# Up projection of a float32 trunk kernel: both parts of hT in one 512-column matmul, the gated product and the rest of gT on VectorE

## The chip, the cores and the metric

The kernel runs on one core of one Trainium2 chip. The metric is device time in microseconds (us). Before the change it is 1369.4 us, the median of three runs (1368.85 to 1369.75).

## The reference

Four residual layers run over 256 tokens of width 1024, all in float32. Each has an attention mixer (three kinds), a gated MLP with a causal depthwise convolution of width 3, and a gate with a per-layer embedding. The change touches the MLP:

```python
D_FF, CONV_WIDTH = 2816, 3
def conv_ffn(h, w_up, conv_w, conv_b, w_down):
    u = h @ w_up                                   # (256, 1024) @ (1024, 5632)
    u = lax.conv_general_dilated(                  # causal, depthwise, width 3
        u, conv_w[:, None, :], window_strides=(1,), padding=[(CONV_WIDTH - 1, 0)],
        dimension_numbers=('NWC', 'WIO', 'NWC'), feature_group_count=2 * D_FF) + conv_b
    gate, up = u[..., :D_FF], u[..., D_FF:]
    return (jax.nn.silu(gate) * up) @ w_down

# in the layer loop
x = x + conv_ffn(rms_norm(x, ffn_norm[i]), w_up[i], conv_w[i], conv_b[i], w_down[i])
```

## The kernel before, in words

Every float32 operand of a matmul is split into two parts, a rounded one (`_hi`, type fp32r) and the rest (`_lo`, the value minus the rounded one). A product is three matmuls into the same PSUM bank: hi by hi, hi by lo and lo by hi.

All weights stand in one list of "units" of 128 x 2048 elements, read in the order of use. SyncE loads them in halves of 128 x 1024 into the ring `w_raw` (4 halves). ScalarE makes `w_hi` of a half (L441, `split_hi`), VectorE makes `w_lo` (L744, `split_lo`), each into a ring of 4 units. While TensorE uses unit u, these two split unit u+4. `lo_ready` tells TensorE that a unit is there and SyncE that a raw half is free. `unit_used` counts the units that TensorE has finished.

The up projection of a layer is 22 up units (`up_unit` on each engine). A unit makes 128 gate columns and 128 up columns of u, transposed, for all 256 tokens: TensorE goes over 2 sides (gate, up) and 8 chunks of the width, with three matmuls of 256 columns for each (L1296 to L1298), 48 in all, the gate's into the first half of one PSUM bank and the up's into the second half. Four banks are used in turn (`up_bank`), so unit u only waits for the convolution of unit u-4 (`conv_done`).

Behind TensorE a unit goes through these steps:

- ScalarE: the last tap with the bias, from PSUM, into `gate_c` (L713) and `up_c` (L715); then the two halves of the split of unit u+4; the silu on `gate_c` (L719); the rounding to `gT_hi` (L721).
- VectorE: the two other taps of the gate and of the up side, from PSUM (L1108, 4 instructions); then two halves of the split of unit u+4.
- GpSimd: the product of `gate_c` and `up_c` (L1282), then the rest, product minus `gT_hi`, to `gT_lo` (L1284).

Each engine works its instructions off in the order of the program. The order around the change is written out by hand; `over_units` turns it into a loop of four units a turn, with the last two units of a layer behind the loop, and with `peel` the first four units are written out ahead of it as well. Inside such a loop counts and addresses come from registers. After the up units the down projection takes 11 units, again with 512-column matmuls (L1320, L1335), on VectorE and ScalarE only splits stand beside it.

Of the kernel before, what the change touches and what calls it, by code (L numbers as in the profile page):

```python
# [17 lines left out]
F32 = mybir.dt.float32  # L18
# [144 lines left out]
def trunk(nc, weights, x_in, p_in, gains, smalls, gainT_in, bf_in, conv, wf_in, rel_in, ident_in, consts_in, out):  # L163
    with ExitStack() as ctx:
# [9 lines left out]
        hT_hi = sb("hT_hi", [P, KC, SEQ], F32R)  # L174
        hT_lo = sb("hT_lo", [P, KC, SEQ], F32R)
# [66 lines left out]
        bank = [ctx.enter_context(nc.psum_tensor(f"bank{i}", [P, 512], F32)) for i in range(8)]  # L242
# [31 lines left out]
        def up_bank(L, slot):  # L274
            return aux[(slot - FIRST_UP[L]) % RING]
# [72 lines left out]
        gainT_ready = sem("gainT_ready")  # L348
        conv_first = sem("conv_first")
# [81 lines left out]
        def _(act):  # L431
# [20 lines left out]

            def split_looped(u, slot, half, k):
                split_hi(u + RING, slot, lambda q: (half(q)[0], half(q)[1] + 2 * RING // RAW))
# [68 lines left out]
            for L in range(DEPTH):  # L523
# [182 lines left out]

                def up_unit(u, slot, half, k):
                    b = slot % 2
                    act.wait_ge(unit_used, u + 1)
                    c = conv_sb[:, L, k, :]  # L710
                    if not isinstance(k, int) or FC * L + k >= 2:
                        act.wait_ge(gT_ready, k + (FC * L - 1))
                    nc.scalar.activation(gate_c[:, b, :], up_bank(L, slot)[:, 0:SEQ], ACT.Identity,  # L713
                                         bias=c[:, 3:4], scale=c[:, 2:3]).then_inc(conv_first, 1)
                    nc.scalar.activation(up_c[:, b, :], up_bank(L, slot)[:, SEQ:2 * SEQ], ACT.Identity,  # L715
                                         bias=c[:, 7:8], scale=c[:, 6:7]).then_inc(conv_first, 1)
                    split_looped(u, slot, half, k)
                    act.wait_ge(conv_done, k + (FC * L + 1))
                    nc.scalar.activation(gate_c[:, b, :], gate_c[:, b, :], ACT.Silu).then_inc(silu_done, 1)  # L719
                    act.wait_ge(prod_done, k + (FC * L + 1))  # L720
                    nc.scalar.activation(gT_hi[:, k, :], gate_c[:, b, :], ACT.Copy).then_inc(gT_hi_ready, 1)  # L721

                act.preload_act_table(ACT.Silu)
                over_units(act, FIRST_UP[L], FC, up_unit, peel=L == 0)
# [11 lines left out]
        def _(dve):  # L736
# [19 lines left out]
            def split_looped(u, slot, half, k):  # L756
                split_lo(u + RING, slot, half)
# [83 lines left out]
            for L in range(DEPTH):  # L841
# [254 lines left out]

                def up_unit(u, slot, half, k):
                    b = slot % 2
                    c = conv_sb[:, L, k, :]

                    dve.wait_ge(conv_first, k * 2 + (2 * FC * L + 2))
                    for tap in (1, 0):
                        lag = 2 - tap
                        for side, buf in ((0, gate_c), (1, up_c)):
                            if tap == 0:

                                dve.wait_ge(conv_tap, k * 2 + (2 * FC * L + side + 1))
                            ins = nc.vector.scalar_tensor_tensor(  # L1108
                                buf[:, b, lag:SEQ], up_bank(L, slot)[:, side * SEQ:side * SEQ + SEQ - lag],
                                c[:, 4 * side + tap:4 * side + tap + 1], buf[:, b, lag:SEQ], ALU.mult, ALU.add)  # L1110
                            if tap == 1:
                                ins.then_inc(conv_tap, 1)
                    ins.then_inc(conv_done, 1)
                    split_looped(u, slot, half, k)

                over_units(dve, FIRST_UP[L], FC, up_unit)
# [10 lines left out]
        def _(pool):  # L1127
# [41 lines left out]
            for L in range(DEPTH):  # L1169
# [108 lines left out]

                def up_unit(u, slot, half, k):
                    b = slot % 2  # L1280
                    pool.wait_ge(silu_done, k + (FC * L + 1))
                    nc.gpsimd.tensor_tensor(gate_c[:, b, :], gate_c[:, b, :], up_c[:, b, :], ALU.mult).then_inc(prod_done, 1)  # L1282
                    pool.wait_ge(gT_hi_ready, k + (FC * L + 1))
                    nc.gpsimd.tensor_tensor(gT_lo[:, k, :], gate_c[:, b, :], gT_hi[:, k, :].bitcast(F32), ALU.subtract).then_inc(gT_ready, 1)  # L1284

                over_units(pool, FIRST_UP[L], FC, up_unit)
# [6 lines left out]
        def _(pe):  # L1293
# [60 lines left out]
            for L in range(DEPTH):  # L1354
# [326 lines left out]
```

## Time and profile before

| what | us |
|---|---|
| median of 3 runs | 1369.4 |
| the profiled execution | 1371.7 |
| its span, first to last instruction | 1369.9 |
| TensorE matmul busy, whole span | 1317.6 (96%) |
| VectorE busy | 971.1 (71%) |
| ScalarE busy | 828.6 (60%) |
| GpSimd busy | 417.6 (30%) |
| up projection of the first layer, 149.6 to 276.5 | 126.9 |

The busy time of an engine is what its instructions took, without waits. The granted TensorE clock is a share of full speed. Matmuls overlap each other in the trace (one of 256 columns is shown as 0.28 us long, and the next starts 0.12 us after it), so the pace of TensorE is read from the starts, not from the durations. On VectorE and ScalarE the start of an instruction can lie up to 0.1 us before the shown end of the one ahead of it, too.

### The profile page before, as it was taken

To read this page: it belongs to the slowest core of one execution; us is meant where nothing else is said; L and a number is where in the kernel's file an instruction comes from. 1 tells how busy PE (TensorE), PEld (TensorE's weight loads), DVE (VectorE), ACT (ScalarE), POOL (GpSimd) and SP (SyncE) were. 2 spreads that over 40 slices of the span, in tenths; PEclk is the share of its full clock that TensorE was granted. 3 is DMA by queue.
4 is the path that set the end of the run, shared out by engine and by line. 5 is a ranking of instruction groups with operands and counts; after the bars stand their busy time and mean duration, and the time that the engine had idled before them with its cause. 6 is when DMAs were issued, how large, how long until landed. Compare 5 with 4: busy or idle time off the path is not lost.

```text
span 1369.9 us, 24686 instructions
## 1 busy us (share of the span) xinstructions
PE 1317.6 (96%) x8340; PEld 1174.1 (86%) x8340; DVE 971.1 (71%) x1531; ACT 828.6 (60%) x1469; POOL 417.6 (30%) x523
## 2 busy tenths in 40 slices
PE   5999999999999999999996799999999999999998
PEld 4878999988788899998875689998887788999887
DVE  4677877755777777774588687776476787777635
ACT  4676666644568666663465666665365786666533
POOL 3541233310265123330037313332014520333200
PEclk9999999999999999999998899999999999999999
DMA  8533655555664456656543155556556335555651
GB/s 289 165 129 102 206 184 182 181 194 177 198 226 136 151 177 184 184 184 201 174 156 108 47 170 184 184 184 194 175 177 200 123 110 184 182 181 179 195 184 62
DMA packets 64311, 232.89 MB, mean 170 GB/s; under 512 B 7312, under 2 KB 7440, under 8 KB 64240
## 3 DMA queue, kind: packets, MB, share of 16 engines
q1 hardware_dynamic: 61344, 221.87, 50.1%
q0 software_dynamic: 2896, 10.08, 2.6%
q8 instruction: 44, 0.72, 0.2%
q14 instruction: 27, 0.22, 0.1%
HBM read 230.87 MB, written 1.05 MB: 169 GB/s over the span
## 4 chain that ended last, share of the span: by engine, by line
PE 80%; DVE 9%; ACT 4%; POOL 3%; issue 2%; DMA 2%; SPq 0%; POOLq 0%; DVEq 0%; ACTq 0%
PE bank L1320 23%; PE bank L1296 17%; PE bank L1297 16%; PE bank L1298 16%; DVE w_lo L744 4%; PE bank L1335 3%; DMA w_raw<-weights 2%; PE bank L1465 2%; PE bank L1488 1%; DVE tok L787 1%; ACT w_hi L441 1%; ACT tok L464 1%; ACT hT_hi L472 1%; PE bank L1385 1%; POOL hrstd L1141 1%
## 5 line engine op out<-in xcount | busy, mean ns | idle before, releaser
L744 DVE TENSOR_TENSOR w_lo<-w_raw,w_hi 128x1024 fp32r<-128x1024 f32 x418 | 556.3, 1367 | 124.3 <-ACT w_hi L441 123.3
L441 ACT ACTIVATE w_hi<-w_raw 128x1024 fp32r<-128x1024 f32 x418 | 422.2, 1056 | 150.4 <-PE bank L1320 117.4
L1296 PE MATMUL bank<-hT_hi,w_hi 128*128 128x256 f32 x1408 | 398.7, 283 | 2.1 <-DVE hT_lo L795 2.1
L1298 PE MATMUL bank<-hT_hi,w_lo 128*128 128x256 f32 x1408 | 398.4, 283 | 0.0
L1297 PE MATMUL bank<-hT_lo,w_hi 128*128 128x256 f32 x1408 | 398.4, 283 | 0.0
L1296 PEld LDWEIGHTS bank<-hT_hi,w_hi 128*128 128x128 f32 x1408 | 270.3, 192 | 3.7 <-issue 3.7
L1298 PEld LDWEIGHTS bank<-hT_hi,w_lo 128*128 128x128 f32 x1408 | 270.3, 192 | 0.0
L1297 PEld LDWEIGHTS bank<-hT_lo,w_hi 128*128 128x128 f32 x1408 | 270.3, 192 | 0.0
L1282 POOL TENSOR_TENSOR gate_c<-gate_c,up_c 128x256 f32<-128x256 f32 x88 | 105.1, 1194 | 288.6 <-ACT gate_c L719 288.6
L1108 DVE SCALAR_TENSOR_TENSOR gate_c<-bank,conv_sb,gate_c 128x255 f32<-128x255 f32 (+1 forms) x176 | 84.1, 478 | 116.6 <-ACT up_c L715 116.6
L1296 PE MATMUL bank<-w_hi,hT_hi 128*128 128x512 f32 (+1 forms) x336 | 135.2, 402 | 7.9 <-DVE w_lo L744 4.2
L1297 PE MATMUL bank<-w_lo,hT_hi 128*128 128x512 f32 (+1 forms) x336 | 130.8, 389 | 0.0
L1298 PE MATMUL bank<-w_hi,hT_lo 128*128 128x512 f32 (+1 forms) x336 | 130.6, 389 | 0.0
L1146 POOL TENSOR_TENSOR ssq<-ssq 128x1 f32<-128x1 f32 x24 | 7.5, 315 | 378.5 <-ACT tok L464 378.5
L721 ACT ACTIVATE gT_hi<-gate_c 128x256 f32 (+1 forms) x88 | 36.8, 419 | 122.2 <-POOL gate_c L1282 122.2
L1284 POOL TENSOR_TENSOR gT_lo<-gate_c,gT_hi 128x256 f32 (+1 forms) x88 | 84.4, 959 | 63.5 <-ACT gT_hi L721 63.5
L1320 PE MATMUL bank<-w_hi,gT_hi 128*128 128x512 f32 x320 | 98.6, 389 | 0.0
L1320 PE MATMUL bank<-w_lo,gT_hi 128*128 128x512 f32 x320 | 98.6, 389 | 0.0
L1320 PE MATMUL bank<-w_hi,gT_lo 128*128 128x512 f32 x320 | 98.5, 389 | 0.0
L713 ACT ACTIVATE gate_c<-bank,conv_sb 128x256 f32<-128x256 f32 x88 | 49.7, 565 | 67.1 <-PE bank L1298 67.1
L1296 PEld LDWEIGHTS bank<-w_hi,hT_hi 128*128 128x128 f32 x336 | 63.9, 190 | 24.7 <-DVE w_lo L744 5.9
L1108 DVE SCALAR_TENSOR_TENSOR up_c<-bank,conv_sb,up_c 128x255 f32<-128x255 f32 (+1 forms) x176 | 83.3, 474 | 0.1
(159 smaller groups left out, 2096.8 us busy)
## 6 DMA issues: line engine op xcount, KB each, us to landing
w_raw<-weights SPq DMA_DIRECT2D x418, 512.0 KB, 4.1
gain<-gains POOLq DMA_DIRECT2D x11, 512.0 KB, 4.9
rel<-rel_in POOLq DMA_DIRECT2D x8, 256.0 KB, 3.6
x<-x_in SPq DMA_DIRECT2D x2, 512.0 KB, 6.3
p_raw<-p_in POOLq DMA_DIRECT2D x4, 256.0 KB, 5.2
out<-x SPq DMA_DIRECT2D x4, 256.0 KB, 2.6
gain<-gains SPq DMA_DIRECT2D x1, 512.0 KB, 6.8
consts<-consts_in POOLq DMA_DIRECT2D x1, 392.0 KB, 3.6
```

The lines of the kernel that those rows point to most:

```text
L441: nc.scalar.activation(w_hi[:, slot, q * HALF:(q + 1) * HALF], w_raw[:, raw, :], ACT.Copy).then_inc(hi_ready, 1)
L713: nc.scalar.activation(gate_c[:, b, :], up_bank(L, slot)[:, 0:SEQ], ACT.Identity, bias=c[:, 3:4], scale=c[:, 2:3]).then_inc(conv_first, 1)
L721: nc.scalar.activation(gT_hi[:, k, :], gate_c[:, b, :], ACT.Copy).then_inc(gT_hi_ready, 1)
L744: nc.vector.tensor_tensor(w_lo[:, slot, cols], w_raw[:, half(q)[0], :], w_hi[:, slot, cols].bitcast(F32), ALU.subtract).then_inc(lo_ready, 1)
L1108: ins = nc.vector.scalar_tensor_tensor(buf[:, b, lag:SEQ], up_bank(L, slot)[:, side * SEQ:side * SEQ + SEQ - lag], c[:, 4 * side + tap:4 * ...
L1282: nc.gpsimd.tensor_tensor(gate_c[:, b, :], gate_c[:, b, :], up_c[:, b, :], ALU.mult).then_inc(prod_done, 1)
L1284: nc.gpsimd.tensor_tensor(gT_lo[:, k, :], gate_c[:, b, :], gT_hi[:, k, :].bitcast(F32), ALU.subtract).then_inc(gT_ready, 1)
L1296: nc.tensor.matmul(out_ap, l_hi, r_hi, start=start, stop=False, skip_group_check=True)
L1297: nc.tensor.matmul(out_ap, l_hi, r_lo, start=False, stop=False, skip_group_check=True)
L1298: return nc.tensor.matmul(out_ap, l_lo, r_hi, start=False, stop=stop, skip_group_check=True)
L1320: last = nc.tensor.matmul(banks[2 * t + b][:, :], l[:, c, ts], w[:, slot, col:col + 512], start=(c == 0 and l is left_hi and w is w_hi), s ...
L1335: last = nc.tensor.matmul(banks[2 * t + b][:, :], l[:, c, ts], w[:, slot, col:col + 512], start=False, stop=(j == 1 and l is left_lo), ski ...
```

## The change

The two parts of hT become one tile `hT` of [128, 8, 2, 256]. For each side and chunk one matmul of 512 columns multiplies `w_hi` with both parts at once: the first 256 columns of the bank get hi by hi, the last 256 hi by lo. A second matmul of 256 columns adds `w_lo` by `hT_hi` to the first 256. A unit is then 32 matmuls and fills two banks, so that two units instead of four fit into the four banks. ScalarE copies the last 256 columns of both banks to `cross_c`, VectorE adds the first 256 of both (`both_c`), and the taps read `both_c` in SBUF. TensorE waits for the sum of unit u-2 (`up_sum`). The product and the rest of gT go from GpSimd to VectorE, and with the rounding on ScalarE they stand in the turn of the next unit.

```diff
+        hT = sb("hT", [P, KC, 2, SEQ], F32R)
+        hT_hi, hT_lo = hT[:, :, 0, :], hT[:, :, 1, :]
+            cross_c = sb("cross_c", [P, 2, SEQ], F32, ffn)
+            both_c = sb("both_c", [P, 2, SEQ], F32, ffn)
...
-        def up_bank(L, slot):
-            return aux[(slot - FIRST_UP[L]) % RING]
+        def up_banks(L, slot):
+            b = 4 + 2 * ((slot - FIRST_UP[L]) % 2)
+            return psum[:, b:b + 2, :]
... ScalarE
+                def round_g(b, count, k):
+                    act.wait_ge(prod_done, count)
+                    nc.scalar.activation(gT_hi[:, k, :], gate_c[:, b, :], ACT.Copy).then_inc(gT_hi_ready, 1)
                 def up_unit(u, slot, half, k):
                     b = slot % 2
                     act.wait_ge(unit_used, u + 1)
+                    if not isinstance(k, int) or FC * L + k >= 1:
+                        act.wait_ge(up_sum, k + FC * L)
+                    nc.scalar.activation(cross_c[:], up_banks(L, slot)[:, :, SEQ:2 * SEQ], ACT.Copy).then_inc(cross_out, 1)
+                    if not isinstance(k, int) or k:
+                        round_g(1 - b, k + FC * L, k + -1)
+                    split_hi(u + RING, slot, later(half), halves=(0,))
+                    act.wait_ge(up_sum, k + (FC * L + 1))
...
-                    nc.scalar.activation(gate_c[:, b, :], up_bank(L, slot)[:, 0:SEQ], ACT.Identity,
+                    nc.scalar.activation(gate_c[:, b, :], both_c[:, 0, :], ACT.Identity,
...
-                    nc.scalar.activation(up_c[:, b, :], up_bank(L, slot)[:, SEQ:2 * SEQ], ACT.Identity,
+                    nc.scalar.activation(up_c[:, b, :], both_c[:, 1, :], ACT.Identity,
...
-                    split_looped(u, slot, half, k)
+                    split_hi(u + RING, slot, later(half), halves=(1,))
                     act.wait_ge(conv_done, k + (FC * L + 1))
                     nc.scalar.activation(gate_c[:, b, :], gate_c[:, b, :], ACT.Silu).then_inc(silu_done, 1)
-                    act.wait_ge(prod_done, k + (FC * L + 1))
-                    nc.scalar.activation(gT_hi[:, k, :], gate_c[:, b, :], ACT.Copy).then_inc(gT_hi_ready, 1)
... VectorE
+                def product(b, count):
+                    dve.wait_ge(silu_done, count)
+                    nc.vector.tensor_tensor(gate_c[:, b, :], gate_c[:, b, :], up_c[:, b, :], ALU.mult).then_inc(prod_done, 1)
+                def rest_g(b, count, k):
+                    dve.wait_ge(gT_hi_ready, count)
+                    nc.vector.tensor_tensor(gT_lo[:, k, :], gate_c[:, b, :], gT_hi[:, k, :].bitcast(F32),
+                                            ALU.subtract).then_inc(gT_ready, 1)
                 def up_unit(u, slot, half, k):
...
+                    dve.wait_ge(cross_out, k + (FC * L + 1))
+                    nc.vector.tensor_tensor(both_c[:], up_banks(L, slot)[:, :, 0:SEQ], cross_c[:], ALU.add).then_inc(up_sum, 1)
+                    if not isinstance(k, int) or k:
+                        product(1 - b, k + FC * L)
+                    split_lo(u + RING, slot, half, halves=(0,))
+                    if not isinstance(k, int) or k:
+                        rest_g(1 - b, k + FC * L, k + -1)
                     dve.wait_ge(conv_first, k * 2 + (2 * FC * L + 2))
... the four taps, now from both_c
-                    split_looped(u, slot, half, k)
-                over_units(dve, FIRST_UP[L], FC, up_unit)
+                    split_lo(u + RING, slot, half, halves=(1,))
+                over_units(dve, FIRST_UP[L], FC, up_unit, peel=True)
+                last = (FIRST_UP[L] + FC - 1) % RING % 2
+                product(last, FC * (L + 1))
+                rest_g(last, FC * (L + 1), FC - 1)
... GpSimd: up_unit goes
... TensorE
-                    if not isinstance(k, int) or FC * L + k >= RING:
-                        pe.wait_ge(conv_done, k + (FC * L + 1 - RING))
+                    if not isinstance(k, int) or FC * L + k >= 2:
+                        pe.wait_ge(up_sum, k + (FC * L - 1))
...
-                            last = three(up_bank(L, slot)[:, side * SEQ:(side + 1) * SEQ], w_hi[:, slot, col], w_lo[:, slot, col],
-                                         hT_hi[:, c, :], hT_lo[:, c, :], c == 0, c == KC - 1)
+                            into = up_banks(L, slot)[:, side, :]
+                            nc.tensor.matmul(into, w_hi[:, slot, col], hT[:, c, :, :], start=c == 0, stop=c == KC - 1,
+                                             skip_group_check=True)
+                            last = nc.tensor.matmul(into[:, 0:SEQ], w_lo[:, slot, col], hT_hi[:, c, :], start=False,
+                                                    stop=c == KC - 1, skip_group_check=True)
```

On ScalarE, in the first layer, the second up unit before is this (names are output<-input, and what the instruction waits for):

```order
L713 ACTIVATE gate_c<-bank,conv_sb 128x256 [waits unit_used]
L715 ACTIVATE up_c<-bank,conv_sb 128x256
L441 ACTIVATE w_hi<-w_raw 128x1024 [waits unit_used,raw_landed0]
L441 ACTIVATE w_hi<-w_raw 128x1024 [waits raw_landed1]
L719 ACTIVATE gate_c<-gate_c 128x256 [waits conv_done]
L721 ACTIVATE gT_hi<-gate_c 128x256 [waits prod_done]
```

In the changed kernel the same unit on ScalarE is:

```order
L727 ACTIVATE cross_c<-bank 128x512 [waits up_sum,unit_used]
L720 ACTIVATE gT_hi<-gate_c 128x256 [waits prod_done]
L448 ACTIVATE w_hi<-w_raw 128x1024 [waits unit_used,raw_landed0]
L735 ACTIVATE gate_c<-both_c,conv_sb 128x256 [waits up_sum]
L737 ACTIVATE up_c<-both_c,conv_sb 128x256
L448 ACTIVATE w_hi<-w_raw 128x1024 [waits unit_used,raw_landed1]
L741 ACTIVATE gate_c<-gate_c 128x256 [waits conv_done]
```

A copy out of PSUM comes first, the rounding (of the unit before) stands ahead of the first half of the split, and the second half stands behind the taps of ScalarE.

On VectorE the body of the loop over the up units before is this, for one unit (ISA and REGISTER_ALU rows are register steps of the loop):

```order
L1108 ISA [waits conv_first]
L1108 SCALAR_TENSOR_TENSOR gate_c<-bank,conv_sb,gate_c 128x255
L1108 ISA
L1108 SCALAR_TENSOR_TENSOR up_c<-bank,conv_sb,up_c 128x255
L1107 REGISTER_ALU
L1108 ISA [waits conv_tap]
L1108 SCALAR_TENSOR_TENSOR gate_c<-bank,conv_sb,gate_c 128x254
L1108 ISA [waits conv_tap]
L1108 SCALAR_TENSOR_TENSOR up_c<-bank,conv_sb,up_c 128x254
L742 ISA
L744 TENSOR_TENSOR w_lo<-w_raw,w_hi 128x1024 [waits hi_ready]
```

In the changed kernel VectorE's second up unit, written out ahead of the loop, is:

```order
L1133 TENSOR_TENSOR both_c<-bank,cross_c 128x512 [waits cross_out]
L1121 TENSOR_TENSOR gate_c<-gate_c,up_c 128x256 [waits silu_done]
L765 TENSOR_TENSOR w_lo<-w_raw,w_hi 128x1024 [waits hi_ready]
L1126 TENSOR_TENSOR gT_lo<-gate_c,gT_hi 128x256 [waits gT_hi_ready]
L1146 SCALAR_TENSOR_TENSOR gate_c<-both_c,conv_sb,gate_c 128x255 [waits conv_first]
L1146 SCALAR_TENSOR_TENSOR up_c<-both_c,conv_sb,up_c 128x255
L1146 SCALAR_TENSOR_TENSOR gate_c<-both_c,conv_sb,gate_c 128x254 [waits conv_tap]
L1146 SCALAR_TENSOR_TENSOR up_c<-both_c,conv_sb,up_c 128x254 [waits conv_tap]
L765 TENSOR_TENSOR w_lo<-w_raw,w_hi 128x1024 [waits hi_ready]
```

The sum and the product now stand ahead of the first half of the split, and the rest of gT ahead of the taps; before, both halves of the split followed the taps.

## Rows read from the trace of the kernel before

**Rows 1.** The page: busy time by engine, and granted clock in 40 slices.

```profile
PE 1317.6 (96%) x8340; PEld 1174.1 (86%) x8340; DVE 971.1 (71%) x1531; ACT 828.6 (60%) x1469; POOL 417.6 (30%) x523
PEclk9999999999999999999998899999999999999999
```

**Rows 2.** Windows (PE, PEld, DVE, ACT, POOL busy, clock, DMA), up projection, first layer.

```profile
149.60:276.50 126.90, 126.83 (x1057) 126.86 (x1058) 98.89 (x132) 80.86 (x129) 45.03 (x42) 1.00 0.59 184
```

**Rows 3.** Timeline of PE (start, duration): first, middle and last of these up units.

```profile
149.67 0.36 PE L1296 MATMUL bank<-hT_hi,w_hi 128*128 128x256 f32 x1 [0.53 <-DVE hT_lo L795]
...
200.13 0.28 PE L1296 MATMUL bank<-hT_hi,w_hi 128*128 128x256 f32 x1
200.25 0.28 PE L1297 MATMUL bank<-hT_lo,w_hi 128*128 128x256 f32 x1
...
276.45 0.63 PE L1320 MATMUL bank<-w_hi,gT_hi 128*128 128x512 f32 x2
```

**Rows 4.** Timeline of ACT, one up unit inside the loop and the next one's start.

```profile
230.78 0.57 ACT L713 ACTIVATE gate_c<-bank,conv_sb 128x256 f32<-128x256 f32 x1 [0.58 <-PE bank L1298]
231.25 0.56 ACT L715 ACTIVATE up_c<-bank,conv_sb 128x256 f32<-128x256 f32 x1
231.70 2.00 ACT L441 ACTIVATE w_hi<-w_raw 128x1024 fp32r<-128x1024 f32 x2
233.65 0.42 ACT L719 ACTIVATE gate_c<-gate_c 128x256 f32<-128x256 f32 x1
235.48 0.42 ACT L721 ACTIVATE gT_hi<-gate_c 128x256 f32 x1 [1.41 <-POOL gate_c L1282]
236.54 0.56 ACT L713 ACTIVATE gate_c<-bank,conv_sb 128x256 f32<-128x256 f32 x1 [0.64 <-PE bank L1298]
```

**Rows 5.** Timeline of DVE, the same unit.

```profile
231.96 0.48 DVE L1108 SCALAR_TENSOR_TENSOR gate_c<-bank,conv_sb,gate_c 128x255 f32<-128x255 f32 x1 [1.23 <-ACT up_c L715]
232.36 0.47 DVE L1108 SCALAR_TENSOR_TENSOR up_c<-bank,conv_sb,up_c 128x255 f32<-128x255 f32 x1
...
233.54 2.89 DVE L744 TENSOR_TENSOR w_lo<-w_raw,w_hi 128x1024 fp32r<-128x1024 f32 x2
```

**Rows 6.** Timeline of PE, 512-column matmuls of the down projection.

```profile
325.44 0.39 PE L1335 MATMUL bank<-w_hi,gT_hi 128*128 128x512 f32 x1
...
325.67 0.39 PE L1335 MATMUL bank<-w_lo,gT_hi 128*128 128x512 f32 x1
```

**Rows 7.** Groups by line and shape (busy us, mean ns), whole span.

```profile
L441 ACT ACTIVATE w_hi<-w_raw 128x1024 fp32r<-128x1024 f32 x418 | 422.2, 1056 | 150.4 <-PE bank L1320 117.4 <-DMA w_raw<-weights 23.3 <-PE bank L1298 9.4
L472 ACT ACTIVATE hT_hi<-bank 128x512 fp32r<-128x512 f32 x48 | 26.3, 604 | 29.7 <-PE bank L1306 29.7
L839 DVE TENSOR_TENSOR wf_lo<-wf_raw,wf_hi 128x256 fp32r<-128x256 f32 x1 | 0.4, 418 | 0.0
```

**Rows 8.** Timeline of DVE outside the up projection, GpSimd doing nothing.

```profile
139.51 0.68 DVE L764 TENSOR_TENSOR x<-x,bank 128x512 f32<-128x512 f32 x1
140.11 1.22 DVE L744 TENSOR_TENSOR w_lo<-w_raw,w_hi 128x1024 fp32r<-128x1024 f32 x1
141.25 1.38 DVE L764 TENSOR_TENSOR x<-x,bank 128x512 f32<-128x512 f32 x2
142.54 1.41 DVE L787 SCALAR_TENSOR_TENSOR tok<-x,rstd,gain 128x512 f32<-128x512 f32 x2
...
283.21 2.36 DVE L744 TENSOR_TENSOR w_lo<-w_raw,w_hi 128x1024 fp32r<-128x1024 f32 x2 [1.04 <-ACT w_hi L441]
288.65 2.36 DVE L744 TENSOR_TENSOR w_lo<-w_raw,w_hi 128x1024 fp32r<-128x1024 f32 x2 [3.08 <-ACT w_hi L441]
```

**Rows 9.** Windows (columns as in Rows 2) of the third layer's attention.

```profile
725.00:730.00 5.00, 3.90 (x19) 2.62 (x17) 5.00 (x7) 2.49 (x3) 4.60 (x3) 1.00 0.47 143
...
735.00:740.00 5.00, 0.12 (x4) 0.00 (x0) 3.21 (x14) 3.13 (x10) 3.19 (x5) 0.81 0.24 95
740.00:745.00 5.00, 3.97 (x22) 3.35 (x22) 2.80 (x10) 3.26 (x11) 2.53 (x5) 0.50 0.00 0
```

More of the change, by code:

```diff
@@ L173, in trunk @@
         tok = sb("tok", [P, TT, D])
-        hT_hi = sb("hT_hi", [P, KC, SEQ], F32R)
-        hT_lo = sb("hT_lo", [P, KC, SEQ], F32R)
+        hT = sb("hT", [P, KC, 2, SEQ], F32R)
+        hT_hi, hT_lo = hT[:, :, 0, :], hT[:, :, 1, :]
         gain = sb("gain", [P, D])
@@ L239, in sc @@
             return sc_tok[:, slot, :] if slot < 4 else sc_gain[:, slot - 4, :]
-        bank = [ctx.enter_context(nc.psum_tensor(f"bank{i}", [P, 512], F32)) for i in range(8)]
+        psum = ctx.enter_context(nc.psum_tensor("bank", [P, 8, 512], F32))
+        bank = [psum[:, i, :] for i in range(8)]
         acc, aux = bank[:4], bank[4:]
@@ L348, in trunk @@
         gainT_ready = sem("gainT_ready")
+        cross_out = sem("cross_out")
+        up_sum = sem("up_sum")
         conv_first = sem("conv_first")
@@ L451, in split_half, with later @@
                 split_hi(u, u % RING, half_of(u), halves=(j % 2,))
+            def later(half):
+                return lambda q: (half(q)[0], half(q)[1] + 2 * RING // RAW)
             def split_looped(u, slot, half, k):
-                split_hi(u + RING, slot, lambda q: (half(q)[0], half(q)[1] + 2 * RING // RAW))
+                split_hi(u + RING, slot, later(half))
             def square(n, t):
@@ L712, in up_unit @@
                         act.wait_ge(gT_ready, k + (FC * L - 1))
-                    nc.scalar.activation(gate_c[:, b, :], up_bank(L, slot)[:, 0:SEQ], ACT.Identity,
+                    nc.scalar.activation(gate_c[:, b, :], both_c[:, 0, :], ACT.Identity,
                                          bias=c[:, 3:4], scale=c[:, 2:3]).then_inc(conv_first, 1)
-                    nc.scalar.activation(up_c[:, b, :], up_bank(L, slot)[:, SEQ:2 * SEQ], ACT.Identity,
+                    nc.scalar.activation(up_c[:, b, :], both_c[:, 1, :], ACT.Identity,
                                          bias=c[:, 7:8], scale=c[:, 6:7]).then_inc(conv_first, 1)
-                    split_looped(u, slot, half, k)
+                    split_hi(u + RING, slot, later(half), halves=(1,))
                     act.wait_ge(conv_done, k + (FC * L + 1))
                     nc.scalar.activation(gate_c[:, b, :], gate_c[:, b, :], ACT.Silu).then_inc(silu_done, 1)
-                    act.wait_ge(prod_done, k + (FC * L + 1))
-                    nc.scalar.activation(gT_hi[:, k, :], gate_c[:, b, :], ACT.Copy).then_inc(gT_hi_ready, 1)
                 act.preload_act_table(ACT.Silu)
-                over_units(act, FIRST_UP[L], FC, up_unit, peel=L == 0)
+                over_units(act, FIRST_UP[L], FC, up_unit, peel=True)
+                round_g((FIRST_UP[L] + FC - 1) % RING % 2, FC * (L + 1), FC - 1)
                 over_units(act, FIRST_DOWN[L], DOWN_UNITS - DOWN_TAIL, split_looped)
@@ L1108, in up_unit @@
                             ins = nc.vector.scalar_tensor_tensor(
-                                buf[:, b, lag:SEQ], up_bank(L, slot)[:, side * SEQ:side * SEQ + SEQ - lag],
+                                buf[:, b, lag:SEQ], both_c[:, side, 0:SEQ - lag],
                                 c[:, 4 * side + tap:4 * side + tap + 1], buf[:, b, lag:SEQ], ALU.mult, ALU.add)
@@ L1276, in _ @@
                 load_gain(3 * L + 2)
[L1279 to L1286, printed above, removed]
                 norm_rstd(3 * L + 2)
```

## The prediction

> **What bounds the kernel now.** I read the page first: TensorE is busy for 96% of the span at a clock that is full almost everywhere [rows 1], so nothing but TensorE's own work and its few gaps sets the time. The stage that is changed comes next, by windows: in the first layer's up projection TensorE is busy 126.83 of 126.90 us at granted clock 1.00 (2.4 GHz), VectorE 98.89, ScalarE 80.86, GpSimd 45.03 [rows 2]. Then its timeline. A 256-column matmul starts every 0.12 us; the stage runs from 149.67 to 276.45, 126.78 us for 22 units, 5.76 a unit, which is 48 x 0.12 [rows 3]. TensorE has no gap there, so the stage ends when the matmuls end. Last, what stands behind it: ScalarE and VectorE take up one unit each 5.76 us because TensorE delivers it so, ScalarE waiting 0.64 us for TensorE and 1.41 for GpSimd [rows 4], VectorE 1.23 for ScalarE [rows 5]. That slack is what the change draws on: the question is whether the new, longer chain between ScalarE and VectorE still closes within one TensorE unit.
>
> **TensorE's part.** A 512-column matmul starts 0.23 us after the one before (two rows: 325.44, 325.67 [rows 6]); against 0.12 for 256 columns the columns cost 0.11 per 256 and the instruction itself some 0.01. To a finer digit: a down unit has 24 of them and VectorE's splits, which follow it, come 5.44 us apart (283.21, 288.65 [rows 8]), so 0.227 each. That gives 16 x 0.227 + 16 x 0.12 = 5.55 us for a unit in place of 5.76: 0.21 us less, and 18.5 us less over 88 units, if TensorE is never kept waiting.
>
> A rule speaks against even that. By the Trainium skill, page "TensorE: Matmul & The Clock Gate", section "Wait — 56ns, not 53.3ns?", a warm matmul costs its columns at 2.4 GHz and about 2.5 ns more; 16 matmuls saved would then be 0.04 us a unit and 3.5 us in all (an estimate from that page). The trace disagrees: 0.12 us for 256 columns is 13 ns above their 107 ns.
>
> **ScalarE and VectorE: the cycle.** With the new order each unit u passes back and forth between the two in one line, because each engine's queue is strict. I start it where VectorE starts the sum of unit u, and give each step the time until the next can start:
>
> - the sum, 512 columns, one source in PSUM: as `x<-x,bank`, whose follower starts 0.60 later [rows 8]: 0.60
> - the product of unit u-1, 256 columns out of SBUF. The nearest row is a 256-column subtraction of 0.418 us [rows 7]; ScalarE waits for its end: 0.42
> - handing over to ScalarE. Inside the loop a register step stands between wait and operation. `up_c` ends at 231.81 and VectorE's tap starts at 231.96 [rows 4, 5]: 0.15
> - the rounding of unit u-1, 0.42 long, its follower able to start some 0.10 earlier (gate_c is 0.57 long, up_c starts after 0.47 [rows 4]): 0.32
> - the first half's `w_hi`, 1.056 [rows 7], whose end VectorE awaits, and 0.04 for the hand-over: 1.10
> - the first half's `w_lo`, start to next start 1.14 (140.11 to 141.25, GpSimd idle [rows 8]): 1.14
> - the rest of gT of unit u-1: 0.42 less the 0.08 by which a follower starts early (0.68 against 0.60 [rows 8]): 0.34
> - four taps, 231.96 to 233.54 [rows 5]: 1.58. ScalarE's two taps are long done by then: they start when `w_hi` ends and need 1.0 of the 1.48 us
> - the second half's `w_lo`: 1.14. Then the sum of unit u+1 can start.
>
> The sum is 0.60 + 0.42 + 0.15 + 0.32 + 1.10 + 1.14 + 0.34 + 1.58 + 1.14 = 6.79 us. The way over ScalarE is as long: from the end of the last tap 0.04, silu 0.33, the copy to cross_c 0.60 (as `hT_hi<-bank`, 0.604 [rows 7]) and 0.04 put the next sum at 6.74. Where units are written out ahead of the loop, the register step falls away and the cycle is 6.67.
>
> VectorE's own work in it, start to start, is 5.14 us (0.60 + 0.34 + 1.14 + 0.34 + 1.58 + 1.14) and would fit under 5.55. What does not fit is the other 1.65 us (6.79 - 5.14), in which VectorE stands between the product and `w_lo` while ScalarE rounds and makes `w_hi` of half 0; nothing else in VectorE's queue can go ahead. Before, the splits of both engines came after the taps and overlapped. GpSimd, whose 45 us per stage [rows 2] are freed, was never the bound; its going gives VectorE's pair of `w_lo` 2.36 us where it took 2.89 [rows 8, 5], and that is counted above.
>
> So from the second unit on TensorE waits for `up_sum` of unit u-2, and that comes every 6.79 us, not every 5.55. Two banks a unit leave room for two units only.
>
> **The stage.** Unit 1 leaves TensorE at 11.10. Its results reach ScalarE about 0.3 later (unit 0 before: 149.67 + 5.76 = 155.43, and in the loop ScalarE's start lies some 0.3 to 0.5 behind a unit's end), the copy takes 0.60, so sum 1 starts at 12.0. Sum 19 starts 18 cycles later, 3 of 6.67 and 15 of 6.79: 133.9. It takes 0.68, TensorE takes it up 0.15 later and needs 5.55 for unit 21: 140.3 us. Before it was 126.78: 13.5 us more in each of four layers, 54 us.
>
> **What hides the rest.** The two last units' silu, product and rest trail TensorE by up to two cycles, but the down projection's first unit needs only the first two units of gT, and its weights come from splits made in up units 18 to 21. Down unit 2 needs the second half of unit 20, ready about 147; TensorE reaches it at 140.3 + 10.9 = 151.2. Down unit 3 needs unit 21's, about 154 against 156.6. The lag is made good there, where each engine has 3 us spare a unit (VectorE takes 2.36 of 5.44 [rows 8]). Loads ask for less per us than before, so they cost nothing. Copies, norms and attention are unchanged.
>
> The profiled execution has a span of 1369.9 us and was 1371.7 itself, against a median of 1369.4. Its span would be 1424. From the median: 1369.4 + 54 = 1423 us.
>
> **Bounds of the unknown terms.** The trace of before has no tap that reads SBUF. From PSUM a tap's follower starts after 0.40 for 255 columns [rows 5]; the scalar_tensor_tensor out of SBUF has 1.41 - 0.74 = 0.67 for 512 [rows 8]. At 1.05 us per 1000 columns (1.14 for 1024 against 0.60 for 512 [rows 8]) both leave 0.13: no gain. I take 0.39 to 0.40, with 0.45 as the upper end (a whole tap without overlap is 0.47).
>
> The Trainium skill, page "VectorE: DVE Perf Modes", section "The TRN2 errata", has 58 cycles beside the columns out of SBUF and 120 out of PSUM. By it four taps would be 0.26 us shorter, the cycle 6.53 and the time 1404 (an estimate from that page); the rows say otherwise for this form.
>
> Hand-overs run from 0.04 to 0.15, five in the cycle or on its equal branch. Low end: all short and the 256-column operations 0.05 shorter each: cycle 6.5. High end: all long, taps 0.45: 7.15. 72 cycles in all make that -21 and +26 us: 1402 to 1449.
>
> **Rivals.**
>
> *TensorE keeps the bound.* If the cycle closed within 5.55 us, the matmuls' saving would show: 1369.4 - 18.5 = 1351. For it speaks that VectorE's work alone is 5.14. Against it, 1.65 us of waiting that the order forces. Chance 0.04.
>
> *TensorE waits, but the cheaper matmuls pay for it.* The stage is 12.0 + 18 cycles + 0.68 + 0.15 + 5.55, which equals the old 126.78 at a cycle of 6.02. If two of the hand-overs and the start of `w_hi` overlapped so far that 0.77 us fell out of the one wait ahead of `w_lo`, the time would be that of before, 1369. Chance 0.02.
>
> *TensorE's clock falls too.* TensorE would stand still 1.2 us in every 6.8. The trace has a stretch of 3.90 busy in 5 us at clock 1.00, and 0.50 (1.2 GHz) only behind a stretch with 0.12 us of work in five [rows 9]. At 1.2 GHz a unit would take about 11 us, more than the cycle; if a tenth of the stage ran so, 9 units would cost 4.3 more each, 39 us: 1462. Chance 0.05.
>
> *The cycle is longer than I sum.* Loop branches each fourth unit, or a half of a load late now that the halves are asked for apart: 7.3 us gives 1423 + 72 x 0.5 = 1459. Chance 0.06.
>
> **How the numbers follow.** The forecast has 0.83, and its own range is that of the bounds. The low end stands at 1402; the high one I leave at 1449, which leaves the two slow rivals and the two fast ones, 0.17, outside. A difference of 0.2%, 2.7 us, can be told from none. Faster 0.04, same 0.02, slower 0.94.
>
> **What would show it.** In the changed profile the up stage of layer one should be about 140 us, with TensorE busy near 83% in it, waiting once a unit, 1.2 us, for VectorE's `both_c`. VectorE's longest wait should stand before the first `w_lo` of a unit, about 1.6 us, on ScalarE's `w_hi`; the pair's halves should be 1.2 us each; successive `both_c` 6.7 to 6.8 us apart; 512-column matmuls 0.227 apart where they don't wait. The down stage should be as long as before. The forecast is wrong if `both_c` comes each 5.6 us, if TensorE's clock is below 1 in the stage, or if matmuls of a unit take other than 5.55 us.

## The result, and the profile after

The changed kernel takes 1425.6 us, the median of 4 runs (1423.2 to 1429.7), against 1369.6 before: a ratio of 1.040, 95% interval 1.037 to 1.044. It is slower by 56 us; 54 were forecast. The profiled execution was the slowest of the four, 1429.7, with a span (first to last instruction) of 1427.9.

The page of the changed kernel, busy time by engine and granted clock in 40 slices, as in [rows 1]:

```profile
PE 1323.1 (93%) x6932; PEld 1099.8 (77%) x6932; DVE 1035.2 (72%) x1795; ACT 876.8 (61%) x1557; POOL 230.1 (16%) x347
PEclk9999999999999999999998899999999999999999
```

TensorE has 1408 fewer matmuls and a smaller share of busy time; the clock is as before. VectorE's share has hardly risen, 71 to 72%: a reader who looks only at shares finds no engine that could be the new bound. The view of waits (who waited for whom: us in total, times, longest) finds it:

```profile
DVE w_lo L765 <- ACT w_hi L448: 216.3, 160, 3.8
ACT gate_c L741 <- DVE up_c L1146: 110.7, 88, 1.5
ACT gT_hi L720 <- DVE gate_c L1121: 107.6, 88, 1.5
...
PEld bank L1599 <- DVE both_c L1133: 57.4, 49, 1.4
...
PE bank L1599 <- DVE both_c L1133: 41.8, 49, 1.1
```

ScalarE waits for VectorE twice in each of the 88 units, VectorE for ScalarE once in nearly each (the 160 of the first line hold other stages too; 20 lie in the first up stage of 22 units), and TensorE waits for VectorE's sum `both_c`. Each stop of TensorE stands in this view twice, at the weight load and at the matmul behind it: the 49 and 49 are 49 stops. Eleven more are booked on a `w_lo`, but they too end just behind a sum (one at 235.19 behind 235.08) and are waits for it. That makes 60 stops, 15 a layer.

VectorE's timeline, one unit in the loop and the two next sums (start, duration, idle before):

```profile
227.66 0.68 DVE L1133 TENSOR_TENSOR both_c<-bank,cross_c 128x512 f32<-128x512 f32 x1
228.26 0.42 DVE L1121 TENSOR_TENSOR gate_c<-gate_c,up_c 128x256 f32<-128x256 f32 x1
230.21 1.23 DVE L765 TENSOR_TENSOR w_lo<-w_raw,w_hi 128x1024 fp32r<-128x1024 f32 x1 [1.53 <-ACT w_hi L448]
231.35 0.42 DVE L1126 TENSOR_TENSOR gT_lo<-gate_c,gT_hi 128x256 f32 x1
231.69 0.48 DVE L1146 SCALAR_TENSOR_TENSOR gate_c<-both_c,conv_sb,gate_c 128x255 f32<-128x255 f32 x1
232.08 0.48 DVE L1146 SCALAR_TENSOR_TENSOR up_c<-both_c,conv_sb,up_c 128x255 f32<-128x255 f32 x1
...
233.27 1.22 DVE L765 TENSOR_TENSOR w_lo<-w_raw,w_hi 128x1024 fp32r<-128x1024 f32 x1
234.40 0.68 DVE L1133 TENSOR_TENSOR both_c<-bank,cross_c 128x512 f32<-128x512 f32 x1
...
241.23 0.69 DVE L1133 TENSOR_TENSOR both_c<-bank,cross_c 128x512 f32<-128x512 f32 x1
```

ScalarE beside it:

```profile
228.81 0.42 ACT L720 ACTIVATE gT_hi<-gate_c 128x256 f32 x1 [1.26 <-DVE gate_c L1121]
229.13 1.04 ACT L448 ACTIVATE w_hi<-w_raw 128x1024 fp32r<-128x1024 f32 x1
230.08 0.59 ACT L735 ACTIVATE gate_c<-both_c,conv_sb 128x256 f32<-128x256 f32 x1
...
233.38 0.42 ACT L741 ACTIVATE gate_c<-gate_c 128x256 f32<-128x256 f32 x1 [1.27 <-DVE up_c L1146]
233.71 0.58 ACT L727 ACTIVATE cross_c<-bank 128x512 f32<-128x512 f32 x1
```

Read the two as one line: VectorE's product ends at 228.68, ScalarE rounds at 228.81 and makes `w_hi` from 229.13 to 230.17, VectorE makes `w_lo` at 230.21. In those 1.53 us VectorE does nothing. The way once around, from one sum to the next, is what is called the cycle here. In the loop it is by turns about 6.75 and 6.82 us, 6.65 where the units are written out, and 6.77 on average from the second sum of the layer to the twentieth; before, a unit took 5.76 [rows 3 to 5].

TensorE's timeline: the starts of two units and of the first that stops, then the end of a later unit and the start and end of the next:

```profile
182.60 0.39 PE L1599 MATMUL bank<-hT,w_hi 128*128 128x512 f32 x1
...
188.15 0.39 PE L1599 MATMUL bank<-hT,w_hi 128*128 128x512 f32 x1
...
194.22 0.50 PE L1599 MATMUL bank<-hT,w_hi 128*128 128x512 f32 x1 [0.36 <-DVE both_c L1133]
...
227.22 0.28 PE L1601 MATMUL bank<-hT,w_lo 128*128 128x256 f32 x1
228.40 0.50 PE L1599 MATMUL bank<-hT,w_hi 128*128 128x512 f32 x1 [0.90 <-DVE both_c L1133]
...
228.85 0.40 PE L1599 MATMUL bank<-hT,w_hi 128*128 128x512 f32 x1
...
233.80 0.40 PE L1599 MATMUL bank<-hT,w_hi 128*128 128x512 f32 x1
```

For seven units TensorE does not stop: it starts at 154.79, and a unit takes 5.55 us (182.60 to 188.15), as forecast. The first stop is ahead of the eighth unit, at 194.22, and from there on every unit waits for a sum. The first matmul of such a unit starts 0.06 us after the end of the sum (228.34). From 228.85 to 233.80 are 14 pairs of a 512- and a 256-column matmul, 0.354 each; 16 of them would be 5.66 us. So TensorE has two paces here, 0.347 a pair before the first stop and mostly 0.354 behind it, both at granted clock 1.00.

### The profile page after: what moved, and what is told of

The parts are those of the page before. It is cut to its first block, busy times and chain, and to the rows that moved or that the text cites. A ratio compares the mean times of both kernels' runs of the same rounds, so it can differ in the third digit from the quotient of the medians.

```text
span 1427.9 us, 21936 instructions
## 1 busy us (share of the span) xinstructions
PE 1323.1 (93%) x6932; PEld 1099.8 (77%) x6932; DVE 1035.2 (72%) x1795; ACT 876.8 (61%) x1557; POOL 230.1 (16%) x347
## 4 chain that ended last, share of the span: by engine, by line
PE 46%; DVE 26%; issue 10%; ACT 10%; POOL 3%; DMA 2%; ACTq 1%; DVEq 1%; SPq 0%; POOLq 0%
PE bank L1352 22%; DVE w_lo L765 11%; PE bank L1599 4%; PE bank L1328 4%; PE bank L1329 3%; PE bank L1330 3%; DVE gate_c L1146 3%; PE bank L1367 3%; DVE both_c L1133 3%; ACT gate_c L735 2%; DVE up_c L1146 2%; ACT up_c L737 2%; PE bank L1601 2%; ACT w_hi L448 2%; DMA w_raw<-weights 2%
## 5 line engine op out<-in xcount | busy, mean ns | idle before, releaser
L1599 PE MATMUL bank<-hT,w_hi 128*128 128x512 f32 x1408 | 501.6, 400 | 53.6 <-DVE both_c L1133 41.8
L1601 PE MATMUL bank<-hT,w_lo 128*128 128x256 f32 x1408 | 393.4, 279 | 0.0
L1599 PEld LDWEIGHTS bank<-hT,w_hi 128*128 128x128 f32 x1408 | 264.0, 188 | 133.8 <-DVE both_c L1133 57.4
L1601 PEld LDWEIGHTS bank<-hT,w_lo 128*128 128x128 f32 x1408 | 265.5, 189 | 0.0
L1328 PE MATMUL bank<-w_hi,hT 128*128 128x512 f32 (+1 forms) x336 | 136.9, 408 | 9.1 <-DVE w_lo L765 5.3
L1329 PE MATMUL bank<-w_lo,hT 128*128 128x512 f32 (+1 forms) x336 | 132.1, 393 | 0.0
L1330 PE MATMUL bank<-w_hi,hT 128*128 128x512 f32 (+1 forms) x336 | 132.1, 393 | 0.0
L1352 PE MATMUL bank<-w_hi,hT 128*128 128x512 f32 x384 | 107.6, 392 | 0.0
L1328 PEld LDWEIGHTS bank<-w_hi,hT 128*128 128x128 f32 x336 | 64.9, 193 | 26.1 <-DVE w_lo L765 7.0
L1146 DVE SCALAR_TENSOR_TENSOR up_c<-both_c,conv_sb,up_c 128x255 f32<-128x255 f32 (+1 forms) x176 | 84.1, 478 | 0.1
L1146 DVE SCALAR_TENSOR_TENSOR gate_c<-both_c,conv_sb,gate_c 128x255 f32<-128x255 f32 (+1 forms) x176 | 84.1, 478 | 0.0
L1352 PEld LDWEIGHTS bank<-w_hi,hT 128*128 128x128 f32 x384 | 70.9, 188 | 14.8
L1330 PEld LDWEIGHTS bank<-w_hi,hT 128*128 128x128 f32 x336 | 64.8, 193 | 13.7
```

Source lines behind the costliest of these rows:

```text
L1146: ins = nc.vector.scalar_tensor_tensor(buf[:, b, lag:SEQ], both_c[:, side, 0:SEQ - lag], c[:, 4 * side + tap:4 * side + tap + 1], buf[:, b ...
L1328: nc.tensor.matmul(out_ap, l_hi, r_hi, start=start, stop=False, skip_group_check=True)
L1329: nc.tensor.matmul(out_ap, l_hi, r_lo, start=False, stop=False, skip_group_check=True)
L1330: return nc.tensor.matmul(out_ap, l_lo, r_hi, start=False, stop=stop, skip_group_check=True)
L1352: last = nc.tensor.matmul(banks[2 * t + b][:, :], l[:, c, ts], w[:, slot, col:col + 512], start=(c == 0 and l is left_hi and w is w_hi), s ...
L1599: nc.tensor.matmul(into, w_hi[:, slot, col], hT[:, c, :, :], start=c == 0, stop=c == KC - 1, skip_group_check=True)
```

## The experiments

**The order, nothing else.** The changed kernel with two ScalarE steps exchanged:

```diff
+                    split_hi(u + RING, slot, later(half), halves=(0,))
                     if not isinstance(k, int) or k:
                         round_g(1 - b, k + FC * L, k + -1)
-                    split_hi(u + RING, slot, later(half), halves=(0,))
```

> The changed kernel with two ScalarE steps of an up unit exchanged: the first half's w_hi goes ahead of the rounding of the unit before. Same instructions, same banks. Theory (the one wait of VectorE between the product and w_lo makes the cycle): w_hi then runs beside VectorE's sum and product, the cycle is 0.60 + 0.34 + 1.14 + 0.34, some 0.3 of waiting for ScalarE's taps, 1.58 and 1.14, 5.4 us, less than a unit of TensorE (16 pairs at 0.354 in the changed kernel's trace, 5.66). TensorE has no gap again and the kernel is faster than the one before: 1369.5 - 4 x 22 x 0.10 = 1360 us. Rival 'VectorE and ScalarE simply have too much work': the work is the same, so 1425. Rival 'two banks a unit, two units deep': the banks are the same, so 1425.

Measured: 1357.0 us (1353.2 to 1358.2, 5 runs), 0.989 of the kernel before (0.988 to 0.991). Work, banks and instructions are those of the changed kernel, 69 us are gone, and it is 1.1% faster than the kernel before. VectorE's timeline in this kernel, and ScalarE's beside it:

```profile
225.39 0.69 DVE L1133 TENSOR_TENSOR both_c<-bank,cross_c 128x512 f32<-128x512 f32 x1
226.00 0.42 DVE L1121 TENSOR_TENSOR gate_c<-gate_c,up_c 128x256 f32<-128x256 f32 x1
226.34 1.23 DVE L765 TENSOR_TENSOR w_lo<-w_raw,w_hi 128x1024 fp32r<-128x1024 f32 x1
227.48 0.42 DVE L1126 TENSOR_TENSOR gT_lo<-gate_c,gT_hi 128x256 f32 x1
228.18 0.48 DVE L1146 SCALAR_TENSOR_TENSOR gate_c<-both_c,conv_sb,gate_c 128x255 f32<-128x255 f32 x1 [0.28 <-ACT up_c L737]
...
231.04 0.69 DVE L1133 TENSOR_TENSOR both_c<-bank,cross_c 128x512 f32<-128x512 f32 x1
```

```profile
224.76 0.60 ACT L727 ACTIVATE cross_c<-bank 128x512 f32<-128x512 f32 x1
225.25 1.05 ACT L448 ACTIVATE w_hi<-w_raw 128x1024 fp32r<-128x1024 f32 x1
226.56 0.42 ACT L720 ACTIVATE gT_hi<-gate_c 128x256 f32 x1 [0.25 <-DVE gate_c L1121]
```

ScalarE makes `w_hi` from 225.25 to 226.30, beside VectorE's sum and product. The wait ahead of `w_lo` is gone, 0.28 before the taps are left, and sums come 5.65 apart in this layer, at TensorE's pace. Windows of the up stage in this kernel, layers one and three (columns as in [rows 2]):

```profile
150.00:274.00 124.00, 123.48 (x699) 106.83 (x698) 114.94 (x193) 94.77 (x149) 0.00 (x0) 1.00 0.58 190
...
807.00:928.00 121.00, 120.72 (x697) 105.63 (x697) 113.29 (x192) 93.67 (x149) 0.00 (x0) 1.00 0.59 192
```

Neither too much work nor two units of banks costs the 56 us by itself: both are here as in the changed kernel, VectorE is busy 93% of this stage, and TensorE has no stop in it.

**One more instruction where VectorE waits, and where it doesn't.** A product of 256 columns into a spare tile, in the changed kernel. First in the gap:

```diff
+                    nc.vector.tensor_tensor(spare[:], consts[:, 0:SEQ], consts[:, 0:SEQ], ALU.mult)
                     split_lo(u + RING, slot, half, halves=(0,))
```

> The changed kernel with one more VectorE instruction a unit, a product of 256 columns into a spare tile, 0.34 us, between the product and the first half's w_lo. Theory: VectorE stands still 1.53 us there, so it costs nothing: 1425. Rival 'VectorE has too much work': 0.34 x 72 = 24 us more, 1450.

Measured: 1425.5 us (4 runs), as without it. VectorE waits 1.20 in place of 1.53. Then behind the taps:

```diff
                     ins.then_inc(conv_done, 1)
+                    nc.vector.tensor_tensor(spare[:], consts[:, 0:SEQ], consts[:, 0:SEQ], ALU.mult)
                     split_lo(u + RING, slot, half, halves=(1,))
```

> The changed kernel with the spare 256-column VectorE product a unit, but now behind the taps, ahead of the second half's w_lo, where VectorE does not wait. Theory: it lengthens the cycle by its 0.34 to 0.40 us, 18 times a layer: 1425 + 4 x 18 x 0.34 = 1450 (up to 1454). Rival 'ScalarE's branch alone makes the cycle': 1425, as with the instruction in the gap.

Measured: 1449.5 us (4 runs), 24 more. Most sums are 7.07 to 7.15 us apart in place of 6.74 to 6.83. The same instruction costs nothing in one place and its 0.34 us, 18 times in each of four layers, in the other. So the time follows the length of the cycle and not the work of VectorE.

**Product and rest alone.** The new order and VectorE's product, with 48 matmuls into four banks and the taps from PSUM as before:

```diff
-                    nc.scalar.activation(cross_c[:], up_banks(L, slot)[:, :, SEQ:2 * SEQ], ACT.Copy).then_inc(cross_out, 1)
...
-                    nc.vector.tensor_tensor(both_c[:], up_banks(L, slot)[:, :, 0:SEQ], cross_c[:], ALU.add).then_inc(up_sum, 1)
...
-                        pe.wait_ge(up_sum, k + (FC * L - 1))
+                        pe.wait_ge(conv_done, k + (FC * L + 1 - RING))
...
```

> One part of the change alone: product and rest of gT on VectorE one unit behind, in the new order; the up projection in 48 matmuls of 256 columns into four banks as before, no copy, no sum. Theory: the cycle is 0.42 + 0.15 + 0.32 + 1.10 + 1.14 + 0.34 + 1.58 + 1.14 = 6.2 us, 0.43 more than TensorE's 5.76. But a layer has only 22 units and TensorE may be four ahead: unit 21 needs the taps of unit 17, which come at about 16.4 + 16 x 6.2 = 115.4 us, before TensorE gets there at 121. So 1369.5, no change, though the cycle is too long. Rival 'a cycle longer than TensorE's unit costs its difference each time': 0.43 x 72 = 31, 1400.

Measured: 1371.1 us, 1.0006 of before (0.9995 to 1.0017). VectorE's products in its trace and the window of the first up stage:

```profile
243.43 0.42 DVE L1115 TENSOR_TENSOR gate_c<-gate_c,up_c 128x256 f32<-128x256 f32 x1
245.43 1.23 DVE L759 TENSOR_TENSOR w_lo<-w_raw,w_hi 128x1024 fp32r<-128x1024 f32 x1 [1.59 <-ACT w_hi L446]
...
249.61 0.42 DVE L1115 TENSOR_TENSOR gate_c<-gate_c,up_c 128x256 f32<-128x256 f32 x1
```

```profile
149.60:276.50 126.90, 126.37 (x1049) 125.79 (x1048) 94.59 (x161) 76.06 (x123) 0.20 (x1) 1.00 0.54 176
```

The same wait is there, 1.59 us, and the cycle is 6.18, longer than TensorE's 5.76. Yet TensorE is never stopped: four banks and the weight ring let it run ahead of a backlog of 0.42 x 20 = 8 us, and the down projection, where only splits are left, pays it back.

So the depth has its share in the 56 us, though not alone. No run gives the changed kernel room for four units. An estimate from its trace: its last up unit would then wait for its weights and not for a bank; their `w_lo` ends at 282.02 (280.80 and 1.22), and with 5.66 for the unit the stage would be 132.9 us, 6 more than before in place of 13.6.

**The matmuls alone.** 512 columns, copy and sum; product and rest on GpSimd, and the old order behind the taps:

```diff
... ScalarE
+                    split_looped(u, slot, half, k)
                     act.wait_ge(conv_done, k + (FC * L + 1))
                     nc.scalar.activation(gate_c[:, b, :], gate_c[:, b, :], ACT.Silu).then_inc(silu_done, 1)
+                    round_g(b, k + (FC * L + 1), k)
... VectorE: split_looped behind the taps; GpSimd: product and rest as before the change
```

> The other part alone: 512-column matmuls, two banks a unit, the copy to cross_c and the sum, but product and rest on GpSimd and the order behind the taps as before. Theory: ScalarE now has the cycle: copy 0.60, sum 0.72, hand-over 0.15, taps 0.95, two w_hi 1.92, silu 0.42, GpSimd's product 1.41 with its hand-overs, rounding 0.33: 6.5 us. The stage is 12.0 + 18 x 6.5 + 6.4 = 135.4, 8.6 more than before, in four layers 34: 1404 us. Rival 'moving product and rest to VectorE is what costs': 1360 to 1370.

Measured: 1503.6 us, 1.097 of before (1.096 to 1.099): 100 us above the forecast. GpSimd's and VectorE's timelines:

```profile
230.10 2.34 POOL L1312 TENSOR_TENSOR gate_c<-gate_c,up_c 128x256 f32<-128x256 f32 x1 [3.98 <-ACT gate_c L738]
```

```profile
229.49 2.35 DVE L762 TENSOR_TENSOR w_lo<-w_raw,w_hi 128x1024 fp32r<-128x1024 f32 x2
233.51 0.69 DVE L1130 TENSOR_TENSOR both_c<-bank,cross_c 128x512 f32<-128x512 f32 x1 [1.67 <-ACT cross_c L727]
...
241.29 0.69 DVE L1130 TENSOR_TENSOR both_c<-bank,cross_c 128x512 f32<-128x512 f32 x1 [1.66 <-ACT cross_c L727]
```

GpSimd's product, 1.20 us long in the kernel before (its L1282), takes 2.34 here and ends 0.60 us after VectorE's pair of `w_lo` (231.84). The cycle is 7.78 in place of 6.5. Before, the pair itself was the longer, 2.89 [rows 5]; by these lengths GpSimd then got in between its halves.

TensorE now stands still for some 2 us ahead of a unit, and its clock does not stay full. Two units in a row (columns as in [rows 2]):

```profile
218.62:226.40 7.78, 5.91 (x32) 4.89 (x32) 4.62 (x7) 4.27 (x7) 3.05 (x2) 1.00 0.37 117
226.46:234.20 7.74, 7.40 (x32) 6.12 (x32) 4.63 (x7) 4.27 (x7) 3.08 (x2) 0.78 0.43 144
```

The granted clock is 0.78 in the second, the mean of a stretch at 2.4 GHz and one at 1.2, where pairs start 0.64 us apart; before both units TensorE had stopped for about 2 us. It costs no time here: the sums stay 7.78 us apart, since the slow unit ends some 7 us before its own sum is due (233.87 against 241.29), and TensorE only waits less (0.39 us) afterwards.

For the product of GpSimd I put something small between the two `w_lo`:

```diff
                     split_lo(u + RING, slot, half, halves=(0,))
+                    nc.vector.tensor_reduce(spare[:], consts[:, 0:SEQ].rearrange("p (h d) -> p h d", d=64), AX.X, ALU.add)
                     split_lo(u + RING, slot, half, halves=(1,))
```

> The kernel with the matmuls' part alone (product on GpSimd), with a small VectorE sum over 256 columns, one SBUF source, between the two halves of w_lo; nothing else is changed. There GpSimd's product took 2.34 us in place of 1.20, until VectorE's second w_lo was over. Theory 'GpSimd is locked out of SBUF reads by VectorE's two-source instructions standing back to back': the product gets in after the first w_lo, the cycle falls by about 1.1 us, 18 x 4 x 1.1 = 79: 1425. Rival 'GpSimd is slow for another reason': 1503 or more.

Measured: 1419.2 us (4 runs). One instruction more and 84 us less:

```profile
227.86 1.20 POOL L1315 TENSOR_TENSOR gate_c<-gate_c,up_c 128x256 f32<-128x256 f32 x1 [3.79 <-ACT gate_c L739]
```

The product is back at 1.20 us, and it is VectorE's second `w_lo` that is longer now, 1.43. The Trainium skill, page "SBUF — State Buffer", section "Who interferes with whom", says that a VectorE instruction with two SBUF inputs and a GpSimd instruction that reads SBUF exclude each other for a whole instruction. The runs agree, and add that two such VectorE instructions back to back can both pass ahead of a waiting GpSimd. A VectorE instruction with two sources in the same place was not tried, so what lets GpSimd in may be the one source or just a third instruction. Why GpSimd got in between the two before, and in the first kernel of this part didn't, with the same offset of 0.61 us, is open as well.

**How much longer the cycle may be.** The kernel with `w_hi` first, and the spare product behind the taps:

> The kernel with w_hi ahead of the rounding, and the same spare product behind the taps. Its cycle was 5.65 with some 0.13 us of waiting for TensorE in it, so about 5.86 with the product. Theory: TensorE may be ahead by a start of 18.4 us against 22 units of 5.66, so cycles up to (124.5 - 18.4) / 18 = 5.89 cost nothing: 1357, no slower than without. Rival 'each 0.1 us of cycle above TensorE's unit counts in each unit': 0.2 to 0.3 x 88 = 18 to 26 us, 1375 to 1383.

Measured: 1361.3 us (1358.4 to 1362.7, 5 runs), 0.993 of before (0.992 to 0.995). VectorE's sums:

```profile
228.67 0.68 DVE L1134 TENSOR_TENSOR both_c<-bank,cross_c 128x512 f32<-128x512 f32 x1
...
234.49 0.69 DVE L1134 TENSOR_TENSOR both_c<-bank,cross_c 128x512 f32<-128x512 f32 x1
```

The cycle is 5.82, and 4 to 5 us are lost (by the ratios to the kernel before, 5), not 18 to 26. From the rounding of hT to the second down matmuls the stage is 128.65 us in the first two layers, as without the product (128.64). The third is 128.65 against 126.32, but not by the cycle: TensorE has no stop in it, its pairs start 0.353 us apart where the profile without the product has 0.347 in this layer. The start of one pair and of the sixteenth behind it, without the product and with it:

```profile
865.60 0.39 PE L1599 MATMUL bank<-hT,w_hi 128*128 128x512 f32 x1
...
871.14 0.39 PE L1599 MATMUL bank<-hT,w_hi 128*128 128x512 f32 x1
```

```profile
865.30 0.40 PE L1601 MATMUL bank<-hT,w_hi 128*128 128x512 f32 x1
...
870.95 0.40 PE L1601 MATMUL bank<-hT,w_hi 128*128 128x512 f32 x1
```

These are 16 pairs each, 5.54 and 5.65 us. Only the fourth layer, at the quicker pace, meets the limit: TensorE stops ahead of its last two units for 0.05 and 0.2 us, and the stage is 126.82 in place of 126.31. So between the two profiles 0.5 us is the cycle's and 2.3 are TensorE's pace; where the rest of the loss lies wasn't found.

**TensorE's own pace.** `w_hi` first, and a side's matmuls in two groups:

```diff
                         for c in range(KC):
                             ... the 512-column matmul
+                        for c in range(KC):
                             ... the 256-column matmul
```

> The kernel with w_hi ahead of the rounding, and TensorE's matmuls of a side in two groups: the 8 of 512 columns, then the 8 of 256, in place of pairs. In pairs a unit took 5.66 us in layers one and two and 5.54 in three and four. Theory 'going from a 256-column matmul to a 512-column one costs': 8 x 0.227 + 8 x 0.12 a side, 5.55 in all layers, 4 to 5 us less, 1352. Rival 'the pace hangs on something else of the layer': the same 1357.

Measured: 1358.1 us, 0.991 of before (0.990 to 0.993), the same as in pairs. The groups' starts in the first layer:

```profile
227.71 2.00 PE L1599 MATMUL bank<-hT,w_hi 128*128 128x512 f32 x8
229.56 1.12 PE L1603 MATMUL bank<-hT,w_lo 128*128 128x256 f32 x8
230.51 1.78 PE L1599 MATMUL bank<-hT,w_hi 128*128 128x512 f32 x7
```

8 of 512 take 1.85 us, 0.231 each, and 8 of 256 take 0.95: 5.60 a unit, and the sums come 5.59 apart in all four layers. In pairs it is 5.65 in two layers of one profile and 5.55 in the two others, so grouping lies between the two and gains nothing. The two paces of the pairs don't belong to a layer: the third is the quick one without the spare product and the slow one with it, and in the changed kernel every layer begins at 0.347 and changes where TensorE first stops. What chooses the pace wasn't found.

## Why the prediction was right, point by point

**The cycle.** Step by step, forecast and the trace after (227.66 to 234.40): sum 0.60 and 0.60; product 0.42 and 0.42; hand-over 0.15 and 0.13; rounding 0.32 and 0.32; `w_hi` with hand-over 1.10 and 1.08; `w_lo` 1.14 and 1.14; rest 0.34 and 0.34; taps 1.58 and 1.58; second `w_lo` 1.14 and 1.13. Together 6.79 and 6.74. Every price came from a row of the same shape, or a neighbour's. ScalarE's branch was nearly equal as forecast: cross_c ends at 234.29, 0.11 before the sum; at 241.20, where the loop turns over, it is the later one, and the 6.83 up to the sum at 241.23 is its.

**Taps from SBUF.** 0.39 to 0.40 from one to the next (231.69, 232.08), as from PSUM [rows 5]. The 58 against 120 cycles that the prediction cites from the Trainium skill, page "VectorE: DVE Perf Modes", section "The TRN2 errata", don't show in this form.

**The stage.** Forecast 140.3 us in the first layer; TensorE's first up matmul started at 154.79 and the first down matmul at 295.18: 140.4. The second sum started 12.0 us behind the first matmul, as forecast, and 18 cycles later came the twentieth, at 288.67. From the rounding of hT to the second down matmuls the four layers are longer by 13.6, 12.9, 13.0 and 13.2 us, together 52.8 against 54. The profiled span has another 5.1 us ahead of the first up stage: hT is rounded at 150.75 against 145.63, and in the other profiles of this study at 145.7 to 148.7, so that is a difference between executions. The medians are 56.0 us apart; the 3 us beyond the four stages have no cause shown.

**The rest hidden.** Between the stages nothing moved: from the second down matmuls to the next hT 204.5 us against 204.6, 194.5 against 194.4, 213.1 against 213.0.

**Rivals.** TensorE did not keep the bound; it did as soon as one instruction had moved. Its clock did not fall: 1.00 in the stage, with stops of about 1.1 us from the eighth unit on. The rival was not baseless, though: behind stops of 2 us, in the kernel with the matmuls alone, the granted clock fell to 0.78 in some units; there a pair at 1.2 GHz took 0.64 us, so a unit would take 10.2 and not the 11 of the prediction. The cycle was not longer than the sum.

**What was off.** Three statements of the prediction did not hold, and none of them moves the sum.

- TensorE does not wait "from the second unit on". The first two sums come early enough, TensorE loses its lead by some 1.1 us a unit and stops 15 times a layer, from the eighth unit on. The stage is as long as forecast because it was added up along the sums and not along TensorE's stops.
- TensorE was to be busy "near 83%" of the stage; it is busy 127.0 of 140.4 us, 90%. The profile shows matmuls longer than their distance, so its busy time can't be compared with a sum of starts.
- A sign of being wrong was named that "matmuls of a unit take other than 5.55 us". Ahead of the first stop they take 5.55, behind it about 5.66, and the wait costs 1.06 us a unit (227.22 to 228.40, less the usual 0.12), not 1.2. The sign was badly chosen: while the cycle is the longer one, the length of a unit only shifts time between work and waiting.

It counts where TensorE is the bound. With `w_hi` first the saving is 13.5 us and not 18.5. The four stages there are 14.0 us shorter than before, and the two at the slow pace are 2.3 us longer than the two others; at the quick pace in all four it would be 18.7, an estimate from these stages. That 18.5 was forecast for this kernel's matmuls is borne out only at that pace. Either saving is far more than the 3.5 us which the prediction worked out from the Trainium skill, page "TensorE: Matmul & The Clock Gate", section "Wait — 56ns, not 53.3ns?".

## What to carry to other kernels

Where two engines hand one unit back and forth, add up the steps along the queues in their order, not each engine's busy time: here a wait of 1.5 us in the middle of VectorE's queue cost 56 us, and moving one independent step of ScalarE ahead, so that it runs before VectorE needs it, gained 69. A cycle longer than the bound engine's unit costs only what the buffers don't take up before the stage ends, so put its length against the number of units and the depth before fearing it. A step of independent work belongs where its engine would wait for the other, ahead of the step that waits.

## What the runs showed of the hardware that I had not expected

- GpSimd's 256-column product took 2.34 us behind two VectorE `w_lo` back to back and 1.20 with a one-source VectorE instruction of 0.41 us between them; the first cost 84 us of kernel time.
- 512-column matmuls in the up stage start 0.231 us apart, against 0.227 in the down stage [rows 6, 8]; in pairs with 256-column ones a pair takes 0.353 or 0.347 us with the same code and full clock. The pace holds for a whole stage without stops, differs between executions in the same layer, and can change where TensorE stops.
- Stops of 1.1 us in every unit left the granted clock at 1.00; with stops of about 2 us it was 0.77 or 0.78 over some units and 1.00 over the others.
